# Each expert weight in two transfers of 1 MB, with a wait for the second half inside the products

## What is computed

```
def expert_block(args):
    xb, e = args
    hb = jax.nn.silu(xb @ w1[e]) * (xb @ w3[e])
    return hb @ w2[e]
```

## Time and profile before

| | |
|---|---|
| median of three runs | 1469.64 us (1467.89 to 1470.36) |
| profiled execution, its own time | 1469.37 us |
| its span | 1467.6 us |
| TensorE busy | 1396.2 us, 95% |
| VectorE busy | 703.1 us, 48% |
| ScalarE busy | 544.7 us, 37% |
| transfers | 351.98 MB, mean 240 GB/s |

### The profile page before, as it was taken

One profiled execution on the slowest core, in us unless ns is written; L12 is line 12 of the kernel. 1 busy time (PEld: TensorE's weight loads), 2 busy tenths in 40 slices (PEclk: granted clock), 3 DMA queues, 4 the chain that ended last, 5 costly groups with the idle time before them and its releaser, 6 DMA issues.

```text
span 1467.6 us, 25889 instructions
## 1 busy us (share of the span) xinstructions
PE 1396.2 (95%) x11102; PEld 1142.9 (78%) x11102; DVE 703.1 (48%) x1084; ACT 544.7 (37%) x852; POOL 20.5 (1%) x15
## 2 busy tenths in 40 slices
PE   7999998999999999999999979989999988999997
PEld 5899997879766665665666548879999976899996
DVE  6675894546621111111111056866655658665564
ACT  3455764145211111111111144655433447643342
POOL 0000002200000000000000000000000000000000
PEclk9999998999999999999999989999999999999999
DMA  9434432015779999999999992235454621345420
GB/s 392 177 152 172 173 122 110 3 58 234 311 330 422 425 426 426 424 426 426 424 426 425 425 412 77 87 139 206 177 196 170 231 101 71 142 186 202 173 86 29
DMA packets 31473, 351.98 MB, mean 240 GB/s; under 512 B 3088, under 2 KB 3344, under 8 KB 4880
## 3 DMA queue, kind: packets, MB, share of 16 engines
q1 hardware_dynamic: 31232, 349.49, 59.1%
q10 hardware_dynamic: 144, 1.05, 0.2%
HBM read 349.48 MB, written 1.05 MB: 239 GB/s over the span
## 4 chain that ended last, share of the span: by engine, by line
PE 81%; DVE 9%; ACT 4%; DMA 3%; issue 2%; DVEq 0%; ACTq 0%
PE psum L433 79%; DMA ring<-in_w 3%; DVE slot_lo L1780 2%; ACT pages L1196 1%; PE psum L523 1%; ACT mix_hi L1220 1%; DVE pages L1960 1%; PE psum L821 1%; DVE pages L2392 0%; DVE tiny L1728 0%; DVE pages L2297 0%; DVE pages L2330 0%; ACT w_hi L1220 0%; ACT gu_hi L1547 0%; DVE pages L1811 0%
## 5 line engine op out<-in xcount | busy, mean ns | idle before, releaser
L433 PE MATMUL psum<-pages 64*64 64x64 f32 (+11 forms) x3280 | 315.3, 312 | 10.2 <-ACT pages L1196 3.5
L433 PEld LDWEIGHTS psum<-pages 128*64 128x64 f32 (+4 forms) x3280 | 225.1, 153 | 86.6 <-issue 46.3
L433 PE MATMUL psum<-ring,pages 128*64 128x256 f32 (+1 forms) x1556 | 210.2, 423 | 4.2 <-DMA ring<-in_w 4.2
L433 PE MATMUL psum<-x_hi,gu_hi 128*128 128x256 f32 x704 | 199.7, 284 | 0.1
L433 PE MATMUL psum<-x_lo,gu_hi 128*128 128x256 f32 x704 | 199.2, 283 | 0.0
L433 PE MATMUL psum<-x_hi,gu_lo 128*128 128x256 f32 x704 | 199.2, 283 | 0.0
L433 PEld LDWEIGHTS psum<-ring,pages 128*64 128x64 f32 x1556 | 111.1, 137 | 89.0 <-issue 40.5
L1780 DVE TENSOR_TENSOR slot_lo<-ring,mix_hi 128x2048 fp32r<-128x2048 f32 x44 | 101.7, 2314 | 78.9 <-ACT mix_hi L1220 78.8
L433 PEld LDWEIGHTS psum<-x_hi,gu_hi 128*128 128x128 f32 x704 | 134.9, 192 | 2.2 <-DVE x_lo L1767 0.5
L433 PEld LDWEIGHTS psum<-x_lo,gu_hi 128*128 128x128 f32 x704 | 134.9, 192 | 1.6
L433 PEld LDWEIGHTS psum<-x_hi,gu_lo 128*128 128x128 f32 x704 | 134.9, 192 | 0.0
(11 more groups left out here) (227 smaller groups left out, 2198.1 us busy)
## 6 DMA issues: line engine op xcount, KB each, us to landing
ring<-in_w SPq DMA_DIRECT2D x58, 2048.0 KB, 25.7
pages<-in_w SPq DMA_DIRECT2D x38, 2048.0 KB, 26.0
ring<-in_ffn SPq DMA_DIRECT2D x44, 1536.0 KB, 6.2
ring<-in_w_in SPq DMA_DIRECT2D x16, 2048.0 KB, 8.5
ring<-in_e_in SPq DMA_DIRECT2D x3, 2048.0 KB, 39.2
ring<-in_w_pa SPq DMA_DIRECT2D x2, 2048.0 KB, 7.8
ring<-in_w_pb SPq DMA_DIRECT2D x2, 2048.0 KB, 7.9
ring<-in_w_o SPq DMA_DIRECT2D x2, 2048.0 KB, 7.5
```

What stands on the lines that cost most here:

```text
L433: return pe.matmul(o, lhsT, rhs, start=start, stop=stop, skip_group_check=True)
```

## The change

Every load of an expert weight becomes two, for columns 0 to 2047 and 2048 to 4095 of each partition's row. The first half raises the semaphore that the whole did, the second a semaphore of its own for the buffer. Those ten are not new: `REUSED` maps them to semaphores whose use lies in earlier stages, with the count that these have reached. TensorE waits for the second half when it has made half of a weight's products. When a buffer is released has not changed.

```diff
+REUSED = {f"second{n}_landed": old for n, old in enumerate(
+    (("x0_landed", 16), ("x1_landed", 16), ("start_landed", 32), ("ln_in_landed", 16), ("gm_rows_landed", 32),
+     ("mixer_landed", 48), ("wab_split", 1), ("wab_high", 1), ("gate_masked", 1), ("g_ready", 1)))}
...
+            def await_second(v):
+
+                pe.wait_ge(*V(f"second{v % BUFFERS}_landed", 16 * (v // BUFFERS + 1)))
...
                 for k in range(KD):
+                    if v is not None and k == KD // 2:
+                        await_second(v)
...
                 for f in range(FE // P):
+                    if v is not None and f == FE // P // 2:
+                        await_second(v)
...
+                def half_load(b, src, h):
+
+                    s = BUFFER_SLOTS[b]
+                    dst = spare[b][:, h, :] if s is None else ring_slot(s)[:, h * PAGE:(h + 1) * PAGE]
+                    sems = S(f"second{b}_landed") if h else spare_landed[b] if s is None else landed[s]
+                    sp.dma_start(dst, src[:, h * PAGE:(h + 1) * PAGE]).then_inc(sems, 16)
...
-                def load_next(it, u):
+                def load_next(it, u, h):
...
-                    if b in spare:
-                        sp.dma_start(spare[b], halves_of(src)).then_inc(spare_landed[b], 16)
-                    else:
-                        sp.dma_start(ring_slot(BUFFER_SLOTS[b]), src).then_inc(landed[BUFFER_SLOTS[b]], 16)
+                    half_load(b, src, h)
...
                         consumed(it, u)
-                        load_next(it, u)
+                        for h in range(2):
+                            load_next(it, u, h)
```

More of the change, by code:

```diff
@@ L122, in shape_tables @@
     }
+REUSED = {f"second{n}_landed": old for n, old in enumerate(
+    (("x0_landed", 16), ("x1_landed", 16), ("start_landed", 32), ("ln_in_landed", 16), ("gm_rows_landed", 32),
+     ("mixer_landed", 48), ("wab_split", 1), ("wab_high", 1), ("gate_masked", 1), ("g_ready", 1)))}
+REUSED["half_read"] = ("vb_ready", 1)
 def stream_items():
@@ L155, in shared @@
                 return "norm_tokens", 4 * NORMS.index(name[:-7])
+            if name in REUSED:
+                return REUSED[name]
             owner, _, kind = name.partition("_")
@@ L806, in _, with expert_h @@
             act = page(10)[:, 1536:2048].rearrange("p (r s) -> p r s", r=2)
-            def expert_h(r, w, half):
+            def await_second(v):
+                pe.wait_ge(*V(f"second{v % BUFFERS}_landed", 16 * (v // BUFFERS + 1)))
+            def expert_h(r, w, half, v=None):
                 each = KD // len(w)
@@ L822, in expert_t, with expert_y @@
                 return last
-            def expert_y(r, w2):
+            def expert_y(r, w2, v=None):
                 each = FE // P // len(w2)
@@ L863, in expert_pair @@
                     pe.wait_ge(free[r], j + base[r])
-                    expert_h(r, landed_weights(6 * j + 2 * r), 0).then_inc(S("w1_read"), 1)
-                    expert_h(r, landed_weights(6 * j + 2 * r + 1), 1).then_inc(full[r], 1)
+                    v = 6 * j + 2 * r
+                    expert_h(r, landed_weights(v), 0, v).then_inc(S("w1_read"), 1)
+                    expert_h(r, landed_weights(v + 1), 1, v + 1).then_inc(full[r], 1)
                 for r in range(2):
@@ L876, in expert_pair @@
                     pe.wait_ge(free[2 + r], 2 * j + base[2 + r] + 1)
-                    expert_y(r, landed_weights(6 * j + 4 + r)).then_inc(full[2 + r], 1)
+                    expert_y(r, landed_weights(6 * j + 4 + r), 6 * j + 4 + r).then_inc(full[2 + r], 1)
             for j in range(PAIRS):
@@ L2576, in _ @@
                 first_of = lambda i: io[LOADS[i % 6]][2 * (i // 6) + LOAD_OF[i % 6]]
-                halves_of = lambda src: src.rearrange("p (n c) -> p n c", c=PAGE)
+                def half_load(b, src, h):
[3 more added lines that the diff above has]
+                    sp.dma_start(dst, src[:, h * PAGE:(h + 1) * PAGE]).then_inc(sems, 16)
                 spare_free = {1: V("h_split", 8), 4: (full[place["w_pb3"][0]], place["w_pb3"][1]),
@@ L2582, in _ @@
                         sp.wait_ge(*spare_free[i])
-                        sp.dma_start(spare[i], halves_of(first_of(i))).then_inc(spare_landed[i], 16)
+                        for h in range(2):
+                            half_load(i, first_of(i), h)
                         continue
@@ L2589, in _ @@
                         sp.wait_ge(full[b_], n_)
-                    sp.dma_start(ring_slot(s), first_of(i)).then_inc(landed[s], 16)
+                    for h in range(2):
+                        half_load(i, first_of(i), h)
                 base = place["moe_base"]
@@ L2616, in _ @@
                         consumed(it, u)
-                        load_next(it, u)
+                        for h in range(2):
+                            load_next(it, u, h)
                 for u in range(3 * EXPERTS - BUFFERS - 6 * ROUND * rounds):
                     consumed(rounds, u)
-                    load_next(rounds, u)
+                    for h in range(2):
+                        load_next(rounds, u, h)
                 early = moe_end
```

## The result

| | before | after |
|---|---|---|
| median | 1469.83 us (12 runs, 1467.78 to 1473.43) | 1472.12 us (12 runs, 1471.01 to 1475.41) |
| span of the profiled execution | 1467.6 us | 1470.8 us |
| ratio after / before | | 1.0019, 95% interval 1.0012 to 1.0027 |

The change makes the kernel slower by 0.19%, some 2.3 to 2.8 us. The forecast was 1473.0 us within 1468.5 to 1479. The difference is inside the 0.2% that the prediction called "same", near its edge; it is clear of the noise, as 1 lies outside the interval of the ratio.

A forecast was written before the change was run, and what follows sets the result against it. The prediction took the stream of expert weights to bound the expert stage. A slower stream, +5.4 us, less 1.8 us of work behind the last landing gave +3.6 us, hence 1473.0 us, range 1468.5 to 1479.

The forecast's parts named there:

- What bounds: Expert stage, 440 to 880 us: the weight stream sets its end, as TensorE is about 2 us a pair faster.
- Term 1: Stream of expert weights: all in 8 KB pieces and two transfers each, so the last landing comes 5.4 us later.
- other packets: Transfers other than the loop's weights in the same DMA engines, instruction code among them: 6.8 us, taken as unchanged.
- Term 2: End of the expert stage: half the last w2's products, 1.83 us instead of 3.67, stand behind its landing; gain 1.8 us, once.
- the signs that the prediction named: Near 421 GB/s around 600 us, last w2 product 1.8 us behind the last landing, norm 3.6 us later.
- Term 3: 96 new TensorE waits, 86 added SyncE issues, and later `e_lora` and `ln2`: counted as nothing, up to 1 us at the upper end.
- moves with it: TensorE's pause of 7.66 us behind the last scatter starts with a branch and was to move with that branch.
- case D: Other packets fall differently between 8 KB pieces, 2 us either way; the clock near the stage's end returns earlier or later, 1 us.
- A: Rival: the DMA rate doesn't change, so only the 1.8 us gain remains, 1467.8 us; chance 0.14.
- B: Rival: reading 8 KB of every 16 KB, or the second completion, costs more: 0.15 us a weight, net +11, 1481; chance 0.17.
- C: Rival: each half pays part of a lone transfer's 2.4 us; paid in full each time, 206 us, 1676; chance 0.01.
- the rule of the page: About 2.0 us fixed for each transfer beside its bytes; paid in full for each of 86 added transfers, 172 us.

## Why the prediction was right

**What bounds.** Right. The stream of transfers sets the stage: the whole cost of the pieces shows at its end (one transfer in small pieces: +4.9), while TensorE's 90 other waits change nothing that shows. One reading of the earlier trace rows was loose: it is the thirteenth to the twenty-third slice that run at 422 to 426 GB/s, and the twenty-fourth, with 412, reaches from 844 to 881 us, past the end of the experts.

**Term 1, the slower stream: 5.4 us forecast.** The mechanism was right. How good the size was depends on where one reads it. The half of 2.49 us, read from `ln2`, measured 2.48. Where the chain now hangs, at the second landing of the last w3, the loss is 4.8 us: the products behind it start 846.96 - 421.27 = 425.69 us after the first issue, against 842.32 - 421.44 = 420.88. The last landing of all, where the forecast had put it, moved by only 3.5. In the kernel before it came 11.2 us after the landing at 842.3 where two weights take 9.9; after, it didn't (856.84 - 846.93 = 9.9). The landing is that of the slowest of the 16 DMA engines, and in the kernel before that one finished its share of the last w2 1.4 us behind the fifteenth; after, 0.05 us behind it. I read this as other packets in that engine, of whose 6.8 us, taken as unchanged, some 1.3 fell elsewhere; no run tests it. The prediction also priced two causes in one, pieces and completions (4.96 against 4.98). The first is all that the runs can tell.

**Term 2, less work behind the last landing: 1.8 us forecast.** From the products behind the second landing of the last w3 to the norm it is 862.75 - 846.96 = 15.79 us, against 17.78 before: 2.0 less. I had put the gain at the last w2, with the last w3 as a second bound beside it. It is the w3 alone, as the last w2 waits for no landing after the change. Half of its products are 1.7 us; the rest is the wait ahead of the last w2. Before, that w2 started 0.30 us behind the copy that it needs, at 853.62; after, it starts 0.06 us behind it, and so it does in the run with both waits at the start. That is why this run's stage has +4.8, though its w3 stands 5.0 us later than before.

**The two together.** At the last w3 they are 4.8 and 2.0 us. Read at the last landing, as the prediction did, they are 3.5 and 0.7: the norm came 860.10 - 853.49 = 6.61 us behind that landing before and comes 5.91 behind it now. Both terms were too large there and have opposite signs, so the sum, 3.6 forecast and 2.8 measured, is nearer than its parts; that much is luck. Of the signs that the prediction named, 421 GB/s and the direction came true, while the last product of the last w2 is still some 3 us behind the last landing, and not 1.8.

**Term 3, at nothing.** Right for the added issues: more of them are long, the longest takes 6.7 us, and nothing waits for them. Right for the 96 waits. The split of `e_lora` waits 0.49 us for its landing, and the norm is not later for it: the length of the stage is taken at the norm, and the sum of the two terms, 4.8 - 2.0 = 2.8, is that length's change. The pause at the branch, 7.66 us before, was 6.66 after, so "moves with it" was wrong by a microsecond. It cost nothing: the products behind it were not the last to be ready, as the next ones, which need the norm's result, start 11.18 us behind the norm in both kernels.

**Behind the stage** the rest of the span took 607.5 us before and 608.1 after, +0.6, for the same instructions. The granted clock differs between the two there. The stretch from 1100 to 1250 us, before and then after:

```profile
1100.00:1250.00 150.00, 137.59 (x1039) 124.79 (x1039) 94.82 (x156) 75.29 (x149) 0.00 (x0) 0.99 0.39 142
```

```profile
1100.00:1250.00 150.00, 139.11 (x1028) 126.44 (x1026) 95.56 (x157) 73.80 (x147) 0.00 (x0) 0.95 0.39 144
```

TensorE is granted 0.99 and then 0.95 of its full clock there, and has more busy time for fewer instructions. Nearer the stage, where the prediction had its case D, the clock came back later: from 870 to 875 us it was 0.85 before and 0.50 after (the lower of the two levels, 1.2 GHz), behind TensorE's pause of 7.7 and 6.7 us. That the clock makes the 0.6 us isn't shown. The run with only the last pair in halves also has 0.95 from 1100 to 1250 us, and its rest of the span took 606.6 us, less than before. Over all runs this rest took 606.1 to 609.0 us, one execution of each, which is more than most of the gains: that is why a gain of 1 or 2 us of stage is hard to find in a median.

**The rivals.** A (no change of rate) fell with 421 GB/s. B (a cost of the stride, or a dearer completion) fell with the halves contiguous in memory and with a half at 2.48 us. C (a part of a lone transfer's cost for each) fell with two transfers in large pieces. The first half-load of the loop landed 4.9 us after its issue, and a whole one 7.3 us: both have 2.4 us beside their bytes, and none of it shows in a full queue. That is also where the rule of the page "DMA: Bandwidth & Descriptors" of the Trainium skill, in its section on the anatomy of one DMA, has to be read rightly. The section fits its fixed 2.0 us or so to transfers that GpSimd issues, and the prediction applied it to SyncE's. It is near the 2.4 us that a transfer of SyncE's alone shows here, and far from what the 86 added ones cost: about 0.006 us each in the run with two transfers in large pieces.

## What to carry to other kernels

When a stage is bound by a stream of transfers with a full queue, look at what each DMA engine gets: keep the pieces (the contiguous run of one partition) as large as they are, and count a second transfer of 1 MB as free. A finer wait pays only behind the last landings of such a stage, so split only the last weights, and then look which landing binds next, for it moves with each step. Buffers whose halves don't adjoin cost some 0.07 us for each load of 2 MB.

## What the runs showed of the hardware that was not expected

- The time of a full queue of weight transfers depends on the piece: 2 MB took 4.90 us in pieces of 16 KB and 4.95 or 4.96 in pieces of 8 KB. From 500 to 600 us the rates were 427 GB/s with 8 of the 86 loads in pieces of 8 KB, 425 with 25, 420 or 421 with all, and 409 with all in pieces of 4 KB. Two transfers in place of one at the same piece size made no difference that the times show.
- The room in the queue seems to go by pieces, and not by bytes or transfers. When the long issue of the last w2 ended, this much was still to land: before, 853.49 - 815.66 = 37.8 us of stream, or 7.7 weights; after, 856.84 - 832.26 = 24.6 us, or 5.0 weights in ten transfers; with one transfer in small pieces (issued at 816.86 for 10.92 us, landed 39.9 us after its start), 29.0 us, or 5.8 weights in six. By an estimate from these numbers that is 83, 80 and 93 pieces for each DMA engine (before, five of the last eight weights have 8 pieces and three have 16; in the other two kernels all have 16). So smaller pieces mean fewer bytes queued: between issue and landing the last w2 took 46 us before and 31 after. It cost nothing here; I expect that a queue with less behind it could run empty, which no run shows.
